# Part of the shared expert moved from the settle stage into the start of the expert stage, and block counts by a shift

## What is computed

```python
def moe(xt, router_w, router_bias, w1, w3, w2, sw1, sw3, sw2):
    scores = jax.nn.sigmoid(xt @ router_w)
    sel = scores + router_bias                      # 64 experts in 8 groups; 4 groups kept, top 8 experts
    ...
    counts = jnp.bincount(flat_e, length=N_EXPERTS)
    padded = (counts + EBLK - 1) // EBLK * EBLK     # blocks of 128 rows of one expert
    ...
    def expert_block(args):
        tok, e = args
        xb = xpad[tok]
        h = jax.nn.silu(xb @ w1[e]) * (xb @ w3[e])
        return h @ w2[e]
    ...
    shared = (jax.nn.silu(xt @ sw1) * (xt @ sw3)) @ sw2
    return routed + shared
```

## Time and profile before

| | us |
|---|---|
| median of three runs | 2968.63 |
| lowest, highest | 2951.04, 2970.68 |
| profiled execution, its own time | 2947.22 |
| span of its trace | 2945.4 |
| mean granted TensorE clock | 0.951 of full |

### The profile page before, as it was taken

The page is one execution under the profiler, slowest core; times in us unless marked ns, Lnnn a source line. Parts: engine busy times, 40 slices in busy tenths (PEclk is TensorE's granted clock), DMA queues, the critical chain, the costliest instruction groups (busy, mean ns, idle before and its releaser), DMA issues. The chain is left out here.

```text
span 2945.4 us, 50832 instructions
## 1 busy us (share of the span) xinstructions
PE 2604.3 (88%) x11125; PEld 1613.2 (55%) x11126; DVE 1661.6 (56%) x3040; ACT 1308.0 (44%) x2072; POOL 506.6 (17%) x664
## 2 busy tenths in 40 slices
PE   4997999869999999999939798989699999999980
PEld 1443545436666666666614345644466666666650
DVE  1424653647666765656648306935566757665656
ACT  1114652126655654555513104632356656664541
POOL 0000000112222222222200000000122222222222
PEclk9998999989999999999969899999799999999995
DMA  7474001159978977876776301011588888887767
GB/s 279 185 313 135 1 27 58 72 196 351 341 272 304 339 276 273 290 282 239 281 291 214 122 0 61 1 49 72 221 299 331 328 291 326 330 320 268 276 235 294
DMA packets 143455, 651.13 MB, mean 221 GB/s; under 512 B 33556, under 2 KB 40724, under 8 KB 85140
## 3 DMA queue, kind: packets, MB, share of 16 engines
q1 hardware_dynamic: 80156, 423.94, 38.7%
q10 hardware_dynamic: 19704, 139.58, 13.3%
q0 software_dynamic: 43520, 86.68, 8.0%
HBM read 630.04 MB, written 91.32 MB: 245 GB/s over the span
## 5 line engine op out<-in xcount | busy, mean ns | idle before, releaser
L1925 PE MATMUL e_psH<-e_w13h,e_xh 128*128 x1184 | 592.9, 501 | 52.5 <-DVE e_w13l L2108 23.7
L2108 DVE TENSOR_TENSOR e_w13l<-ring,e_w13h x512 | 592.6, 1219 | 41.0 <-ACT e_w13h L2013 37.3
L1951 PE MATMUL e_psY<-ring,e_gt 128*128 x1184 | 564.4, 604 | 5.4 <-ACT e_gt L2026 5.4
L2013 ACT CAST e_w13h<-ring x512 | 497.8, 1042 | 83.2 <-issue 58.2
L1925 PE MATMUL e_psH<-e_w13l,e_xh 128*128 x1184 | 473.3, 400 | 0.0
L2121 DVE TENSOR_TENSOR e_xl<-e_psT,e_xh 128x512 fp32r<-128x512 f32 x296 | 197.8, 688 | 417.8 <-ACT e_xh L2033 269.5
L1911 PE MATMUL e_psT<-ident,e_xg 128*128 128x128 f32 x1184 | 323.2, 275 | 10.2 <-DMA e_xg<-h_rows,e_gidx 6.7
L1925 PEld LDWEIGHTS e_psH<-e_w13h,e_xh 128*128 128x128 f32 x1184 | 227.6, 192 | 169.1 <-issue 131.6
L1931 PE MATMUL e_psH<-e_w13h,e_xl 128*128 x1184 | 307.9, 402 | 0.0
L1951 PEld LDWEIGHTS e_psY<-ring,e_gt 128*128 128x128 f32 x1184 | 213.1, 190 | 162.4 <-issue 150.1
L2033 ACT CAST e_xh<-e_psT 128x512 fp32r<-128x512 f32 x296 | 169.5, 587 | 276.3 <-PE e_psT L1911 149.4
(11 more groups left out here) (295 smaller groups left out, 2872.4 us busy)
## 6 DMA issues: line engine op xcount, KB each, us to landing
ring<-in_exp_w SPq DMA_DIRECT2D x256, 1024.0 KB, 8.3
ring<-in_exp_w ACTq DMA_DIRECT2D x130, 1024.0 KB
p_lead<-in_ada_w SPq DMA_DIRECT2D x40, 1024.0 KB, 6.4
v<-y_rows SPq DMA_DIRECT2D x54, 512.0 KB, 5.3
f_Y<-y_rows SPq DMA_DIRECT2D x12, 1536.0 KB, 16.5
ring<-in_c_w_in SPq DMA_DIRECT2D x6, 2048.0 KB, 9.8
ring<-in_ada_w SPq DMA_DIRECT2D x8, 1024.0 KB, 16.5
ring<-in_sh_w SPq DMA_DIRECT2D x6, 1024.0 KB, 9.1
```

The costliest lines, as they stand in the source:

```text
L1925: nc.tensor.matmul(psH[par][:], xh[par][:, k * P:(k + 1) * P], w[:, bass.DynSlice(half, 1), :, k, :], start=(k == 0 and i == 0), stop=False)
L1951: mm = nc.tensor.matmul(psY[:, c * 512:(c + 1) * 512], gt[par][:, k * P:(k + 1) * P], raw2[:, bass.DynSlice(half, 1), k, c * 512:(c + 1) * ...
L2013: nc.scalar.copy(w13h[:, bass.DynSlice(half, 1), :, k, :].rearrange("p o u k n -> p (o u) (k n)"), raw13[:, bass.DynSlice(half, 1), :, k, ...
L2108: nc.vector.tensor_tensor(low, raw, high.bitcast(F32), ALU.subtract).then_inc(w13_lo, 1)
```

## The change

- A number `late` is set per layer: 2 in layer 0, 1 in layer 1. The shared expert of the last `late` row tiles is no longer computed in settle, but in experts. The other tiles (`early`: four in layer 0, three in layer 1) stay.
- The transposed rows of the late tiles are kept in a new buffer `s.hold`, which outlives settle. The mixers' buffers `proj`, `rot`, `wide`, `share` and one of `prob` become parts of it.
- The shared weights move from ring slots 0 and 1 to slots 1 and 2. The expert stage loads the first expert into slot 0 at once, and the second expert's weights only when the shared products have read slots 1 and 2.
- In settle, the first two shared gates stand later in VectorE's chain, gate 2 behind the counts, gate 3 behind the table; block ends and the table's transposes follow `early - 2` in place of 2.
- Block counts: add 127, keep as integers, shift right by 7.
- The index table `slots` is made by GpSimd (iota) and no longer loaded.
- In experts, the late tiles' products, gates, copies and stores stand between the first lists, the first gather and the first weight splits, with waits of SP, ScalarE, VectorE and TensorE on them.

```diff
@@ shared weights, settle
+def shared_weights(s):
+    return (s.ring[:, 1, :].rearrange("p (k n) -> p k n", k=KD),
+            s.ring[:, 2, KF * D:2 * KF * D].rearrange("p (k n) -> p k n", k=KF))
...
     n_t = len(tiles)
+    early = n_t - r.late
...
-        HT = sb("r_HT", [P, KD, T])
+        HT = sb("r_HT", [P, KD, early * P])
+        HL = s.hold[:].rearrange("p (i k n) -> p i k n", i=r.late, k=KD)
...
-        w13 = s.ring[:, 0, :].rearrange("p (k n) -> p k n", k=KD)
-        w2 = s.ring[:, 1, 0:KF * D].rearrange("p (k n) -> p k n", k=KF)
+        w13, w2 = shared_weights(s)
...
             up_products(0)
-            for i in range(n_t):
-                if i + 1 < n_t:
+            for i in range(early):
+                if i + 1 < early:
                     up_products(i + 1)
-                if i == 2:
+                if i == early - 2:
                     block_ends()
                 down_products(i)
                 if i == 0:
                     positions()
-                if i == 2:
+                if i == early - 2:
                     turn_table()
...
             link(nc.vector.tensor_tensor(gs[:], best[:, :, 0], best[:, :, 1], ALU.add))
-            shared_gate(0)
...
             link(nc.vector.tensor_tensor(mflat, mflat, pen[:].unsqueeze(2).to_broadcast([P, n_t * NG, EG]), ALU.add))
-            shared_gate(1)
+            shared_gate(0)
...
             nc.vector.tensor_copy(maskb[:], mask[:]).then_inc(mask_ready, 1)
+            shared_gate(1)
...
-            if n_t > 2:
-                shared_gate(2)
...
-            for j in range(KMAX):
-                link(nc.vector.tensor_scalar(cmpT[0:E, j, :], psZ[0:E, 384:512], float(j * P), None, ALU.is_gt))
-                link(nc.vector.tensor_scalar(cmp[:, j, :], psT[:, 512:512 + E], float(j * P), None, ALU.is_gt))
-            link(nc.vector.tensor_copy(neT[0:E, :], cmpT[0:E, 0, :]))
-            with nc.allow_low_precision("counts up to 6 are exact"):
-                nc.vector.tensor_reduce(nbT[0:E, :], cmpT[0:E].rearrange("p j n -> p n j"), AX.X, ALU.add).then_inc(nb_ready, 1)
-            link(nc.vector.tensor_reduce(nb[:], cmp[:].rearrange("p j n -> p n j"), AX.X, ALU.add))
-            shared_gate(3)
+            link(nc.vector.tensor_scalar(cntT[0:E, :], psZ[0:E, 384:512], float(P - 1), None, ALU.add))
+            link(nc.vector.tensor_scalar(cnt[:], psT[:, 512:512 + E], float(P - 1), None, ALU.add))
+            link(nc.vector.tensor_scalar(neT[0:E, :], psZ[0:E, 384:512], 0.0, None, ALU.is_gt))
+            link(nc.vector.tensor_scalar(some[:], psT[:, 512:512 + E], 0.0, None, ALU.is_gt))
+            link(nc.vector.tensor_scalar(cntT[0:E, :], cntT[0:E, :], SHIFT, None, ALU.logical_shift_right))
+            nc.vector.tensor_copy(nbT[0:E, :], cntT[0:E, :]).then_inc(nb_ready, 1)
+            link(nc.vector.tensor_scalar(cnt[:], cnt[:], SHIFT, None, ALU.logical_shift_right))
+            link(nc.vector.tensor_copy(nb[:], cnt[:]))
+            shared_gate(2)
...
             link(nc.vector.tensor_copy(r.table[0:1, 0:last], psT[0:1, 0:last]))
-            for i in range(4, n_t):
+            for i in range(3, early):
                 shared_gate(i)
@@ experts, SP
-            sp.dma_start(slots[:], a["k_slots"]).then_inc(slots_in, 16)
             n = sp.value_load(r.table[0:1, last + 3:last + 4], min_val=4, max_val=E // 2)
             load13(0, 0)
+            sp.wait_ge(sh_up, r.late)
             load13(1, 1)
+            for i in range(r.late):
+                sp.wait_ge(sh_y, i + 1)
+                at = (n_t - r.late + i) * P
+                sp.dma_start(s.yrows[l][at:at + P, TOPK, :], ysb[i][:]).then_inc(sh_out, 16)
@@ experts, GpSimd
+            nc.gpsimd.iota(slots[:], [[1, P * (KMAX + 1)]], base=0, channel_multiplier=0,
+                           allow_small_or_imprecise_dtypes=True).then_inc(slots_ready, 1)
@@ experts, TensorE
+            def shared_up(i, lists):
+                for k in range(KD):
+                    mm = nc.tensor.matmul(psH[i][:], HL[:, i, k, :], sh_w13[:, k, :], start=(k == 0), stop=(k == KD - 1))
+                    if k == KD - 1:
+                        mm.then_inc(sh_up, 1)
+                    if k in lists:
+                        index(lists[k], lists[k] % 2, code[lists[k]])
+            def shared_down(i):
+                pe.wait_ge(sh_g, i + 1)
+                if i:
+                    pe.wait_ge(sh_gt, i)
...
+                pe.wait_ge(sh_gt, i + 1)
+                if i:
+                    pe.wait_ge(sh_y, i)
...
             code = codes(pe, 0, 6)
-            for b in range(4):
-                index(b, b % 2, code[b])
+            if r.late == 2:
+                shared_up(0, {3: 0})
+                shared_up(1, {3: 1, 7: 2})
+            else:
+                shared_up(0, {3: 0, 7: 1})
+            shared_down(0)
+            if r.late == 1:
+                index(2, 0, code[2])
             for k in range(KD):
                 turn(0, 0, 0, k)
+            index(3, 1, code[3])
+            if r.late == 2:
+                shared_down(1)
             step(0, 0, 0, None, code[0], code[4], True)
+            pe.wait_ge(sh_y, r.late)
             step(1, 1, 1, code[0], code[1], code[5])
@@ experts, ScalarE
+            load2(0, bass.DynSlice(expert_at(act, 0), 1), slice(0, 1))
+            shared_silu(0)
+            if r.late == 1:
+                shared_turned(0)
             split13(0, code[0])
+            if r.late == 2:
+                shared_silu(1)
+                shared_turned(0)
+                shared_rows(0)
             rows_in(0, 0)
+            if r.late == 2:
+                shared_turned(1)
+            shared_rows(r.late - 1)
+            act.wait_ge(w2_in, 16)
+            act.sem_inc(act_clear, 1)
+            load2(1, bass.DynSlice(expert_at(act, 1), 1), slice(1, 2))
             split13(1, code[1])
+            act.wait_ge(sh_g, r.late)
             step(0, 0, 0, code[0], code[2])
+            act.wait_ge(sh_out, 16 * r.late)
             step(1, 0, 1, code[1], code[3])
@@ experts, VectorE
-            dve.wait_ge(slots_in, 16)
-            for b in range(5):
-                choose(b, b % 2, code[b])
-                if b:
-                    indices(b - 1)
+            dve.wait_ge(slots_ready, 1)
+            choose(0, 0, code[0])
+            choose(1, 1, code[1])
+            indices(0)
+            choose(2, 0, code[2])
+            if r.late == 2:
+                shared_gate(0)
+            indices(1)
+            choose(3, 1, code[3])
+            if r.late == 1:
+                shared_gate(0)
             rest13(0, code[0])
+            if r.late == 2:
+                indices(2)
+                choose(4, 0, code[4])
+                shared_gate(1)
+            else:
+                indices(2)
+                choose(4, 0, code[4])
             rows_in(0, 0)
+            indices(3)
             rest13(1, code[1])
+            dve.wait_ge(sh_turned, r.late)
             step(0, 0, code[0], code[2], code[5])
```

More of the change, by code:

```diff
@@ L42 @@
 KMAX = NTOK // P
+SHIFT = 7
 NEG = -1e30
@@ L255, in project @@
             mrow = [sb(f"p_mrow{i}", [P, 512]) for i in range(2)]
-        proj = [sb(f"proj{i}", [P, 512]) for i in range(2)]
-        rot = [sb(f"rot{i}", [P, 512]) for i in range(2)]
+        proj = [s.hold[:, i * 512:(i + 1) * 512] for i in range(2)]
+        rot = [s.hold[:, D + i * 512:D + (i + 1) * 512] for i in range(2)]
         norm = sb("p_norm", [P, 512])
@@ L1357, in settle @@
         res1 = sb("r_res1", [P, n_t, E])
-        cmpT = sb("r_cmpT", [P, KMAX, P])
+        cntT, cnt, some = sb("r_cntT", [P, P], I32), sb("r_cnt", [P, E], I32), sb("r_some", [P, E])
         nbT, neT = sb("r_nbT", [P, P], BF16), sb("r_neT", [P, P], BF16)
-        cmp = sb("r_cmp", [P, KMAX, E])
         nb, ne = sb("r_nb", [P, E]), sb("r_ne", [P, E])
@@ L1478, in logits @@
                 for k in range(KD):
-                    mm = nc.tensor.matmul(psZ[:, i * E:(i + 1) * E], HT[:, k, i * P:(i + 1) * P], rw[:, k, :], start=(k == 0), stop=(k == KD - 1))
+                    mm = nc.tensor.matmul(psZ[:, i * E:(i + 1) * E], turned(i)[:, k, :], rw[:, k, :], start=(k == 0), stop=(k == KD - 1))
                 mm.then_inc(z_mm, 1)
@@ L1504, in up_products @@
                 for k in range(KD):
-                    mm = nc.tensor.matmul(psH[i % 2], HT[:, k, i * P:(i + 1) * P], w13[:, k, :], start=(k == 0), stop=(k == KD - 1))
+                    mm = nc.tensor.matmul(psH[i % 2], turned(i)[:, k, :], w13[:, k, :], start=(k == 0), stop=(k == KD - 1))
                 mm.then_inc(h_mm, 1)
@@ L1578, in copy_rows @@
                 act.wait_ge(t_mm, turn_no["h", i] + 1)
-                nc.scalar.copy(HT[:, :, i * P:(i + 1) * P], psT[:].rearrange("p (k n) -> p k n", k=KD)).then_inc(t_copied, 1)
+                nc.scalar.copy(turned(i), psT[:].rearrange("p (k n) -> p k n", k=KD)).then_inc(t_copied, 1)
             nc.scalar.preload_act_table_set(LN_EXP)
@@ L1729, in _ @@
```

(36 more changed lines are left out.)

28 lines of the change are left out of this document (22 added, 6 removed).

## The result

The changed kernel takes 2939.41 us (median of 20 runs, 2926.14 to 2968.32), the kernel before 2963.02 beside it (20 runs, 2944.97 to 2984.40): a ratio of 0.9923, 95% interval 0.9906 to 0.9940, so 18 to 28 us faster, 23.6 by the medians: 0.8%, under the 1% that the prediction took for what a measurement can tell. The profiled execution took 2937.98 us against 2947.22.

A forecast was written before the change was run, and what follows sets the result against it. TensorE's pace was taken to bound the expert stages, so earlier starts shorten the kernel: 16.7 us (layer 0) + 15.6 (layer 1) = 32.3, less 3, gives 29 off 2963.4: 2934 us, range 2914 to 2958.

The forecast's parts named there:

- Settle: End of settle: last copy 23.2 us sooner in layer 0, 10.8 us in layer 1, as shared tiles leave.
- The new counts: Settle's block counts by shift: 1.5 us ahead of the semaphore instead of 5.2, 3.6 saved, hidden in layer 0.
- TensorE's start: Layer 0 expert stage: shared product 0 starts at 602.9 us, 3.5 us behind the first transfer at 599.4.
- Block 0: First block product of the expert stage: 9.7 us sooner in layer 0, 7.6 us sooner in layer 1.
- the two waits: Layer 1, before the first block product: 2.1 us for gate 0 and 1.5 us for the fourth list's indices.
- Rival 3: Start of the expert stages: the clock stays low through the shared products; 10 us slower, 2973, or 3002; chance 0.07.
- What follows the start: First to third block product: weight waits and low clock go, 5.4 + 1.6 us in layer 0; 2.25, 4.2, 1.6 in layer 1.
- the sum: Both layers' expert starts: 16.7 + 15.6 = 32.3 us, less 3 for late hand-overs, 29 us.
- rival 1: Third block product: weights bind, a load taking 11.5 us instead of 8.3; gain 18 us or less, 2945; chance 0.28.
- The new wait that I had feared in layer 1: Layer 1 expert start: gate 0's 2.1 us wait could make the clock fall, costing 1.6 us.
- the signs set down: Expert stage starts: transfers 23 and 11 us sooner, full clock from the first block, no weight wait at the third.
- Rival 2: Later in both expert stages: weight waits of 8.5 us a layer thin out; gain 46 us, 2917; chance 0.15.

The follow-up runs named there:

- the free SyncE: Changed kernel with the shared rows' stores issued from ScalarE's queue, so SyncE no longer waits for them: 2938.34 us, ratio to before 0.9913.
- spread: Changed kernel, TensorE's loop reading one or two codes ahead of each block and down product, not seven at each round's head: 2919.65 us, ratio to before 0.9842.

## Why the prediction came out right, step by step

**Settle.** 23.2 and 10.8 us forecast, 23.5 and 11.3 measured. In layer 0 tile 3's products stood behind the table copy and the gate as worked out: TensorE waits 1.17 us at 591.73. The new counts ran 1.6 us to the semaphore, 1.5 forecast; the comparisons' price, 3.6, came out at 3.9. The 10.8 rested on it.

**TensorE's start.** Forecast 602.9 from before's times; after's common point lies 2.05 us later, so 604.95: measured 604.78. Only the first transfer came later than forecast, 5.4 us behind the last copy and not 3.8: it is now a load of weights, and SyncE reads its registers ahead of it, as it did in before ahead of the same load.

**Block 0.** 9.7 us forecast in layer 0, 12.3 measured: between the start and block 0 lie 26.1 us, not 28.5. The low clock took less: the window 606 to 608 was granted 0.56 and the next 1.00, so 3 us of work at the low level, 1.5 us lost instead of 2.5. The lists and turns took less as well: the eight turns and the fourth list lie between 625.18 and 626.22, 1.0 us, and the three other lists take about 0.15 each of TensorE's time (the second up product begins 0.15 behind the first list, 609.77 and 609.92): 1.5 us, where I had 2.7 from the earlier trace rows. In layer 1 7.6 forecast, 7.9 measured, and the two waits that I put in at 2.1 and 1.5 are there, 1.89 and 2.04. Rival 3 (the clock stays low) did not come.

**The step that failed is "What follows the start".** It held 15 of the sum's 32.3 us. It took the 2.54 us ahead of the third block for waiting for weights, which an earlier load would end, and with it went the clock's dip behind it, in both layers: 7.0 and 8.05 us. Measured from block 0 to block 2: layer 0 24.70 in before, 26.99 in after, 2.3 longer and not 7.0 shorter; layer 1 24.14 and 21.61, 2.5 shorter: 0.2 us in both together. The waits there now are 3.03 and 2.27. Two things stand in the place of that step. The wait is TensorE's own read of the codes: it stayed with lighter weights, grew by 3.7 with a second read and went when the read was spread. The name in the bracket was the last event by the profile before the product, not what held it: the low halves of the third block were ready 6.5 us earlier, and the view of the source line, which I had read for the stage's start, would have shown the load at 661.2. The second thing is an order that I had not priced. Weights 2 were not late by the sum: issued at 635 and landed at 643 to 646 on after's clock (forecast plus the 2.05 us), measured 633.99 and 645.2. But ScalarE's copy of block 0's gate stands behind their split, and the down product waits for that copy: 2.82 us at 649.62, which the sum didn't have. The load took 11.2 us from issue to split, near the 11.5 of rival 1, with the shared rows' stores beside it; its length and its issue both carry on to the third block, by this path (2.6 us by lighter weights, 3.1 by the free SyncE).

**The clock.** It fell behind waits again, as the earlier trace rows had it, and at shorter ones (windows of 2 us: TensorE busy, granted clock, DMA share, GB/s):

```profile
606.00:608.00 2.00, 2.00 (x3) 0.56 1.03 434
608.00:610.00 2.00, 2.00 (x12) 1.00 0.98 414
660.00:662.00 2.00, 2.00 (x8) 0.50 1.02 428
2090.00:2092.00 2.00, 2.00 (x7) 0.50 1.00 395
2110.00:2112.00 2.00, 2.00 (x7) 0.50 0.25 102
```

The last two lie behind the 2.04 us wait of the fourth list and the 2.27 of the third block. The new wait that I had feared in layer 1, gate 0's, took 1.89 us, and the windows behind it stayed at 1.00; the fourth list's did the harm in its place. Nor did the clock fall behind the longer wait of 2.82 us in layer 0:

```profile
650.00:652.00 2.00, 1.60 (x4) 1.00 0.95 401
656.00:658.00 2.00, 0.17 (x1) 1.00 1.00 418
```

So the length of the wait just ahead doesn't decide alone; what does, these rows don't show. The Trainium skill (TensorE: Matmul & The Clock Gate, section "HAM oscillation — how this bites in real kernels") has a TensorE that waits between bursts come back at the low clock; the three waits of 2.04, 2.27 and 3.03 us agree, those of 1.89 and 2.82 don't. In before the clock was low from block 0 on as well, 5.7 us in layer 0 and 8.4 in layer 1. In after layer 0 has none of it, and layer 1 some 3.4 us, behind the fourth list: 5 us less at half speed are worth 2.5 us, as much as layer 1's stretch is shorter.

**The sum.** 29 us forecast of 2963.4, 2934; measured 23.6 (18 to 28) of 2963.0, 2939.4. The marks give 12.3 + 7.9 at the two blocks 0 and 20.4 at blocks 3. What separates 20.4 from 23.6 is inside the scatter and stays open. That the number came so near is in part luck: the two starts gave 2.9 us more than forecast, 3 us had been taken off as a reserve, and the 15 us of the failed step came out as nothing. 2939.4 lies as near to rival 1's 2945 as to the forecast, and the range, 44 us wide for the scatter, would have held a gain of 5 us. A gain of over 1% had the larger chance, 0.54 against 0.42 for within 1%; it was 0.8%. Of the signs set down, the first transfers came 21.9 and 9.9 us sooner (23 and 11 forecast), and the clock stood at 1.00 from block 0 on in layer 0 only, until the third block; the wait of over 2 us at the third block, the sign for rival 1, was there with another cause. Rival 2, thinner waits later in the stage, did not come: those ahead of block products went from 19.5 us to 23.6 in the 690 us.

## What to carry to other kernels

Work moved past a barrier pays as far as it fills a stretch in which the main engine waits, and its gain is to be read at the first block, then again two blocks on, where the next order of queues takes part of it. A wait that is named after another engine should be checked against the waiting engine's own instructions that aren't counted as busy: if it stays when the named cause is made cheaper, it was never that. At the head of a loop on the bounding engine, register reads are paid in every round; reading two codes less gave here, in the measured medians, about as much as the whole change.

## What the runs showed of the hardware

- A read of seven table entries into TensorE's registers takes a load of 1.70 to 3.3 us (median 1.93 in 690 to 1380 us of after) and seven moves that begin 0.3 us apart; a single one takes a load of 0.30 us (median, spread). A second read of seven delays the third block by 3.7 us in layer 0 and 3.0 in layer 1.
- Single waits of 2.04, 2.27, 2.54 and 3.03 us on TensorE were followed by a window at 0.50 of the clock, those of 1.89 and 2.82 us weren't; a second read in every round brought the mean of a steady stretch from 1.00 to 0.88.
- Eight small integer and comparison operations on 64 or 128 columns took 2.0 us in all, six of them 1.6; the table of 128x896 slots made on GpSimd 0.88 us by the profile.
